# Layers written out, six parts of output, level products round the row groups: one change to a two-layer encoder step on Trainium2

## The reference

```python
def trunk_layer(x, ...):
    x = layer_norm(ALPHA * x + 0.5 * swiglu(x, w_ffn1_in, w_ffn1_out), g[0], b[0])
    mix, ... = token_mixing(x, ...)
    x = layer_norm(ALPHA * x + mix, g[1], b[1])
    x = layer_norm(ALPHA * x + memory_attend(x, mem_k, mem_v, w_q, w_o), g[2], b[2])
    return layer_norm(ALPHA * x + 0.5 * swiglu(x, w_ffn2_in, w_ffn2_out), g[3], b[3])

def token_mixing(x, ...):          # one projection x @ w_in feeds all three branches
    y_pool = pool_mixer(...)       # trailing means over 2, 4, 8, 16 tokens
    y_mla  = ...                   # 8 heads of attention over compressed keys, block-causal mask
    y_gla  = gla_mixer(...)        # 4 heads of 32: gated linear attention, A = sum q * decay * k
    m = g_a * (y_pool @ w_a) + g_b * (y_mla @ w_b) + g_c * (y_gla @ w_c)
    return m @ w_out

def swiglu(x, w_in, w_out):
    gate, up = split(x @ w_in)     # inner width 2816
    return (silu(gate) * up) @ w_out
```

## Time and profile before

| | |
|---|---|
| median of 3 runs | 3059.01 us (3057.55 to 3063.16) |
| profiled execution | 3057.24 us, span 3055.5 us |
| granted TensorE clock, mean | 0.989 of full speed |
| busy, share of the span | TensorE 96%, GpSimd 36%, VectorE 35%, ScalarE 30% |
| chain that ended last | TensorE 88%, VectorE 5%, ScalarE 2%, issue 2% |
| DMA | 259.8 MB, mean 85 GB/s |

### The profile page before, as it was taken

One profiled execution on the slowest core, in us unless ns is written; L12 is line 12 of the kernel. 1 busy time (PEld: TensorE's weight loads), 2 busy tenths in 40 slices (PEclk: granted clock), 3 DMA queues, 4 the chain that ended last, 5 costly groups with the idle time before them and its releaser, 6 DMA issues.

```text
span 3055.5 us, 54729 instructions
## 1 busy us (share of the span) xinstructions
PE 2936.7 (96%) x22374; PEld 2813.5 (92%) x22374; DVE 1069.3 (35%) x1864; ACT 917.1 (30%) x1404; POOL 1087.8 (36%) x454
## 2 busy tenths in 40 slices
PE   7999999899999999999999999999999999999996
PEld 7999998699998799999999999877999988999995
DVE  3111245643435461112331121566434254511123
ACT  2222243322334252222332221533223342422223
POOL 3343323034362234434333434321333622333431
PEclk9999999999999999999999999999999999999998
DMA  3222222022252022222222222211222511222222
GB/s 140 90 83 89 90 76 81 22 78 84 83 194 76 30 82 90 83 88 90 77 87 88 84 90 88 75 64 36 78 83 85 199 56 53 73 89 89 83 90 85
DMA packets 74436, 259.80 MB, mean 85 GB/s; under 512 B 10704, under 2 KB 13648, under 8 KB 72848
## 3 DMA queue, kind: packets, MB, share of 16 engines
q1 hardware_dynamic: 65520, 238.58, 24.1%
q10 hardware_dynamic: 8736, 18.64, 1.7%
HBM read 249.32 MB, written 7.87 MB: 84 GB/s over the span
## 4 chain that ended last, share of the span: by engine, by line
PE 88%; DVE 5%; issue 2%; ACT 2%; DVEq 2%; ACTq 1%
PE PS L320 87%; DVE XL L1320 1%; DVE Y L1320 1%; ACT Y L923 1%; DVEq L1395 0%; DVE PT L1635 0%; DVE SC L1610 0%; ACT LNT L923 0%; ACT WH L923 0%; DVE P L1625 0%; DVE O L1323 0%; DVE LNT L1320 0%; DVE LNT L1323 0%; DVEq L1810 0%; PE PS L590 0%
## 5 line engine op out<-in xcount | busy, mean ns | idle before, releaser
L310 POOL TENSOR_TENSOR WL<-WR,WH 128x1024 fp32r<-128x1024 f32 x450 | 1087.6, 2423 | 1911.4 <-ACT WH L923 1911.0
L320 PE MATMUL PS<-XH,WH 128*128 128x272 f32 x4192 | 927.1, 292 | 49.3 <-DVE XL L1320 40.3
L320 PE MATMUL PS<-XL,WH 128*128 128x272 f32 x4192 | 915.6, 290 | 0.0
L320 PEld LDWEIGHTS PS<-XH,WH 128*128 128x128 f32 x4192 | 679.3, 189 | 68.8 <-DVE XL L1320 52.4
L923 ACT ACTIVATE WH<-WR 128x1024 fp32r<-128x1024 f32 x455 | 479.6, 1056 | 726.7 <-DMA WR<-in_w 708.0
L320 PEld LDWEIGHTS PS<-XL,WH 128*128 128x128 f32 x4192 | 680.1, 190 | 0.0
L320 PE MATMUL PS<-XH,WL 128*128 128x272 f32 x4192 | 651.2, 289 | 0.0
L320 PEld LDWEIGHTS PS<-XH,WL 128*128 128x128 f32 x4192 | 576.7, 189 | 0.0
L1320 DVE TENSOR_TENSOR LNT<-LNT,PS 128x544 f32<-128x544 f32 x88 | 63.4, 721 | 796.1 <-PE PS L320 759.0
L923 ACT ACTIVATE LNT<-PS 128x544 f32<-128x544 f32 x138 | 85.9, 622 | 719.4 <-PE PS L320 719.2
L320 PE MATMUL PS<-HL,WH 128*128 128x272 f32 x1408 | 299.1, 289 | 0.0
(11 more groups left out here) (222 smaller groups left out, 2849.5 us busy)
## 6 DMA issues: line engine op xcount, KB each, us to landing
WR<-in_w SPq DMA_DIRECT2D x455, 512.0 KB, 3.5
Y<-in_x ACTq DMA_DIRECT2D x4, 544.0 KB, 11.8
out_y<-Y ACTq DMA_DIRECT2D x1, 2176.0 KB, 6.6
MRAW<-in_mem ACTq DMA_DIRECT2D x2, 1024.0 KB, 4.8
MKs<-in_memk_in ACTq DMA_DIRECT2D x2, 1024.0 KB, 6.0
MVs<-in_memv_in ACTq DMA_DIRECT2D x2, 1024.0 KB, 9.0
out_mem_k<-MKp ACTq DMA_DIRECT2D x2, 1024.0 KB, 6.0
out_mem_v<-MVp ACTq DMA_DIRECT2D x2, 1024.0 KB, 8.0
```

The lines of the kernel that those rows point to most:

```text
L310: pool.tensor_tensor(WL[s][:, :], WR[s][:, :], WH[s][:, :].bitcast(F32), ALU.subtract).then_inc(lo_ready[s], 1)
L320: return pe.matmul(out, lhsT, rhs, start=start, stop=stop, skip_group_check=True)
```

## The change

Seven edits, most of them to the order of the work.

**1. Layers written out.** The outer loops of TensorE, ScalarE and VectorE become Python loops, so that each layer has its own instructions; the inner loops stay. `norm_last(l, 3, 1)` goes from the end of a layer into the `quad` of the next layer's `f1i`; only the last layer's stands alone.

```diff
-            with pe.Fori(0, L) as l:
-                ffn_in(l, "f1i", 4 * l)
+            for l in range(L):
+                ffn_in(l, "f1i", 4 * l, (lambda: norm_last(l - 1, 3, 1)) if l else None)
...
                 ffn_out(l, "f2o", 4 * l + 3, l * 2 + 1)
-                norm_last(l, 3, 1)
+            norm_last(L - 1, 3, 1)
```

```diff
+Y_PARTS = [(0, 0, 4), (0, 4, 4), (1, 0, 4), (1, 4, 2), (1, 6, 1), (1, 7, 1)]
...
-            for s in range(AHEAD):
-                sp.wait_ge(w_used[s], L * ROUNDS + 1)
-                sp.dma_start(WR[s][:, :], io["w"][0, s]).then_inc(landed[s], 16)
+            for h, c, n in Y_PARTS:
+                sp.wait_ge(S["y_fin"], 16 * (4 * L - 1) + 8 * h + c + n)
+                sp.dma_start(io["y"].rearrange("p (c t) -> p c t", c=KC)[:, c:c + n, hs(h)],
+                             Y[:, c:c + n, hs(h)]).then_inc(S["st_y"], 16)
...
-            act.wait_ge(S["y_fin"], 16 * 4 * L)
-            act.dma_start(io["y"], Yf[:, :]).then_inc(S["st_y"], 16)
```

```diff
-            for h in (0, 1):
-                for s in (0, 1) if h == 0 else (2, 3, 4):
-                    convert(0, s)
-                for c in range(KC):
...
+            load_x(0)
+            act.preload_act_table_set("silu_and_others")
+            convert(0, 0)
+            x_hi(0, 0)
+            convert(0, 1)
+            convert(0, 2)
+            load_x(1)
+            x_hi(0, 1)
+            convert(0, 3)
+            convert(0, 4)
+            x_hi(1, 0)
+            x_hi(1, 1)
...
             for i in range(16):
+                for s in {0: (0,), 2: (1,), 4: (2,)}.get(i, ()):
+                    ve.wait_ge(hi_ready[s], 1)
+                    tt(WL[s][:, :], WR[s][:, :], WH[s][:, :].bitcast(F32), ALU.subtract).then_inc(lo_ready[s], 1)
```

```diff
-                    for h in range(4):
-                        r = slice(32 * h, 32 * h + 32)
-                        if sample:
-                            m_ = mm(PS[0:NS, 4 + h, 0:NS], a[r, NP_:T], b[r, NP_:T], True, True)
-                        else:
-                            for i in range(4):
+                    for i in range(1 if sample else 4):
+                        for h in range(4):
+                            r = slice(32 * h, 32 * h + 32)
+                            if sample:
+                                m_ = mm(PS[0:NS, 4 + h, 0:NS], a[r, NP_:T], b[r, NP_:T], True, True)
+                            else:
                                 m_ = mm(PS[:, 4 + h, i * 128:(i + 1) * 128], a[r, i * 128:(i + 1) * 128],
                                         b[r, i * 128:(i + 1) * 128], True, True)
```

```diff
                     act.wait_ge(S["pt_mm"], l * 8 + h + 1)
...
+                    f(PT[:, 0:512], PS[:, 3 * e, :], ACT.Copy)
...
-                    ve.tensor_copy(PT[:, 0:1024].rearrange("p (b t) -> p b t", b=2),
-                                   PS[:, 3 * e:3 * e + 2, :]).then_inc(S["pt_d"], 1)
+                    ve.tensor_copy(PT[:, 512:1024], PS[:, 3 * e + 1, :]).then_inc(S["pt_d"], 1)
...
+                    normalize(h)
+                    if h:
                         out_lo(h - 1)
-                    normalize(h)
```

```diff
                 normalize(0)
-                normalize(1)
                 queries(4)
                 turned(0)
+                normalize(1)
                 queries(5)
...
                 maxima(3)
+                normalize(3)
                 out_lo(2)
-                normalize(3)
                 turned(3)
```

More of the change, by code:

```diff
@@ L294, in _ @@
         def _(sp):
-            with sp.Fori(0, L * ROUNDS) as q:
+            for s in range(SLOTS):
+                sp.wait_ge(w_used[s], 1)
+                sp.dma_start(WR[s][:, :], io["w"][0, s]).then_inc(landed[s], 16)
+            sp.dma_start(TAB[:, :], io["tab"]).then_inc(S["const_in"], 16)
+            sp.dma_start(CST[:, :], io["cst"]).then_inc(S["const_in"], 16)
+            sp.dma_start(LN_[:, 0:1024], io["mask"]).then_inc(S["const_in"], 16)
+            with sp.Fori(1, L * ROUNDS) as q:
                 for s in range(SLOTS):
@@ L298, in _ @@
                     sp.dma_start(WR[s][:, :], io["w"][q, s]).then_inc(landed[s], 16)
-            for s in range(AHEAD):
-                sp.wait_ge(w_used[s], L * ROUNDS + 1)
-                sp.dma_start(WR[s][:, :], io["w"][0, s]).then_inc(landed[s], 16)
+            for h, c, n in Y_PARTS:
+                sp.wait_ge(S["y_fin"], 16 * (4 * L - 1) + 8 * h + c + n)
+                sp.dma_start(io["y"].rearrange("p (c t) -> p c t", c=KC)[:, c:c + n, hs(h)],
+                             Y[:, c:c + n, hs(h)]).then_inc(S["st_y"], 16)
+            sp.wait_ge(S["st_y"], 16 * len(Y_PARTS))
         @block.gpsimd
         def _(pool):
-            with pool.Fori(0, L * ROUNDS) as q:
+            for s in range(FIRST, SLOTS):
+                pool.wait_ge(hi_ready[s], 1)
+                pool.tensor_tensor(WL[s][:, :], WR[s][:, :], WH[s][:, :].bitcast(F32), ALU.subtract).then_inc(lo_ready[s], 1)
+            with pool.Fori(1, L * ROUNDS) as q:
                 for s in range(SLOTS):
@@ L932, in convert, with load_x, x_hi @@
                 f(WH[s][:, :], WR[s][:, :], ACT.Copy).then_inc(hi_ready[s], 1)
[L934 to L949 removed]
+            def load_x(h):
+                for i in (0, 1):
+                    act.dma_start(Y[:, 4 * i:4 * i + 4, hs(h)],
+                                  io["x"].rearrange("p (c t) -> p c t", c=KC)[:, 4 * i:4 * i + 4, hs(h)]).then_inc(
+                        S[f"x_in{2 * h + i}"], 16)
+            def x_hi(h, i):
+                act.wait_ge(S[f"x_in{2 * h + i}"], 16)
+                for c in range(4 * i, 4 * i + 4):
+                    f(XH[:, ch(c, h)], Yf[:, ch(c, h)], ACT.Copy).then_inc(S["x_hi"], 1)
+            load_x(0)
[10 more added lines that the diff above has]
+            x_hi(1, 1)
+            for l in range(L):
                 done = [AHEAD - 1]
@@ L997, in layer_norm @@
                 def layer_norm(n, j, c0):
+                    last = n == 4 * L - 1
                     def rstd(h):
@@ L1008, in chunk @@
                         act.wait_ge(S["ln_d"], 16 * n + 8 * h + c + 1)
-                        f(XH[:, ch(c, h)], Yf[:, ch(c, h)], ACT.Identity, scale=g, bias=b)
+                        if not last:
+                            f(XH[:, ch(c, h)], Yf[:, ch(c, h)], ACT.Identity, scale=g, bias=b)
                         f(Yf[:, ch(c, h)], Yf[:, ch(c, h)], ACT.Identity, scale=g, bias=b).then_inc(S["y_fin"], 1)
@@ L1018, in layer_norm @@
                             square_last(j, 1)
-                        if c == 3:
+                        if c == 3 and not last:
                             hi_to(c0 + 3)
@@ L1023, in layer_norm @@
                         chunk(1, c)
-                        if c == 0:
+                        if c == 0 and not last:
                             hi_to(c0 + 4)
@@ L1028, in ffn_out @@
                     c0 = CBASE[name]
+                    ahead = min(c0 + 24, L * CHUNKS - 1 - l * CHUNKS)
                     for c in range(20):
-                        hi_to(c0 + c + 4)
+                        hi_to(min(c0 + c + 4, ahead))
                         for m in range(KC - 1):
@@ L1033, in ffn_out @@
                                 square(n, m)
-                    hi_to(c0 + 24)
+                    hi_to(ahead)
                 def proj_out(l, name, n):
@@ L1396, in layer_norm @@
                         mul(h, c)
-                        if c:
+                        if c and not last:
                             lo(h, c - 1)
@@ L1402, in layer_norm @@
                             head(1)
-                    lo(h, KC - 1)
+                    if not last:
+                        lo(h, KC - 1)
             ve.memset(XH[:, KC * T:].bitcast(F32), 0.0)
@@ L1419, in _ @@
             ve.drain()
-            with ve.Fori(0, L) as l:
+            for l in range(L):
                 def gated(b, x):
```

14 lines of the change are left out of this document (2 added, 12 removed).

## The result

The changed kernel takes **2979.68 us** (median of 4 runs, 2978.99 to 2980.57) against 3060.07 us before (median of 4, 3057.55 to 3063.16): a ratio of 0.9739, 95% interval 0.9727 to 0.9751, 80.4 us less. The forecast was 2977 us, with a range of 2964 to 2997. The total is close, and hides one term that was almost wholly wrong.

The account below looks back on a forecast made before the run. TensorE, busy 2936.7 of 3055.5 us, was taken as the bound. Terms summing to 82.1 us came off the profiled 3057.2 us, and 1.8 us was added for the median: 2977 us, range 2964 to 2997.

Parts of the forecast that it names:

- Level products: 16 level calls: changing head after every matmul lets row groups overlap, 1.5 us saved a call, 24.0 us, bounds 0 and 26.
- The rival of pairs: Level calls: only two row groups run together, so 10.9 us gained instead of 24.0, total 2990 us; chance 0.16.
- Attention: Attention over heads: earlier normalising and a copy split between VectorE and ScalarE save 12.4 us, bounds 6 and 15.
- The rival that the ring closes elsewhere: Attention keeps its length: a head's cycle from scores to next scores is held elsewhere, waits only renamed; 2989 us, chance 0.11.
- Memory: Memory stage: earlier low-part subtraction removes 7.7 us of waits and 4.2 us lost at low clock, less 0.6: 11.3 us.
- the two bank releases that now stand behind the subtraction: Memory stage: releases formerly behind VectorE's low-part subtraction, which moves behind the fifth chunk; may cost 0.3 us each.
- Cross attention: Cross attention: waits for the fifth query group's copy, 5.6 us, and the last head's weights, 3.2 us, go: 8.8 us.
- Turn: Between the layers: without the loop, 34.05 us becomes 31.86 as where sums are woven into the next stage; 2.2 us.
- Head: Kernel start: earlier weight conversions and low parts let TensorE start at 13.4 instead of 20.50 us; 7.0 us, bounds 5 and 8.5.
- Tail: Kernel end: first half 3.8 us earlier, last normalisation 4.9 us less, output in parts 4.3 less; 13.0 us, bounds 11 and 14.
- Slower by reading code: Rival: reading in the second layer's code starves TensorE; at 10 ns a matmul more than the gain is lost, 3089 us; chance 0.02.
- Clock: Half-clock stretches after two level calls and in the second layer's attention and cross attention: half of 6.8 us, 3.4 us gained.

Follow-up runs that it names:

- woven copies: Changed kernel with VectorE's first two memory-key copies moved into its gaps waiting for ScalarE in chunks 6 and 7: 2971.3 us, 8.3 less than the changed kernel.
- the order by pairs: Changed kernel with level products alternating between heads 0 and 1 through all four blocks, then heads 2 and 3: 2987.0 us, 7.3 more than the changed kernel.

## Why the prediction was right, and where it was wrong

- **Level products: right in mechanism, the size a little low.** Taken were 1.5 us a call, measured 1.64 in each of 16, 26.3 us, the upper bound. 1.1 us a layer is given back at one place that the forecast had called free of waits: behind the first call TensorE now waits 0.84 us for ScalarE, which the longer call had covered.

```profile
640.12 0.52 PE L337 MATMUL PS<-BH,WH 128*128 128x272 f32 x2 [0.84 <-ACT LNT L940]
```

  The two stretches at half the clock behind level calls, 1.5 us each, are gone and lie in this row: 26.3 - 2.2 + 3.0 = 27.1, and 0.2 in the products between. The rival of pairs falls: four groups run side by side. The ratio of 3.07 times from the Trainium skill, "TensorE: Matmul & The Clock Gate", section "Part 3: Packing small matmuls", is not reached by this trace: the call's length fell by 2.82 / 1.17 = 2.4 times, with 128 columns where the page has 512. Nor did the strict order that the section states lead to two at a time: in the new order the records of four groups start 7 ns apart in the trace.
- **Attention: right in the whole, one part too large.** 12.4 forecast, 13.5 measured, of which 1.9 is what the second layer gained more than the first; before had a stretch at half the clock there. The order of normalising is 7.0 us when undone (7). The copy is 5.8 in the medians (5.5), but some 4 in the trace, where the low parts give back 1.8 us: the forecast named them as late next and priced them only in its lower bound. The wait before the values is 1.20 us (1.1 forecast). The rival that the ring closes elsewhere falls for these edits; with the whole copy on ScalarE the waits do change their name to the low parts.
- **Memory: wrong, 2.1 instead of 11.3 us.** The step that failed is the price of "the two bank releases that now stand behind the subtraction", 0.3 us each. It priced what the subtraction adds to the releases, and not how late they are against the time at which TensorE would want the bank: without the old wait it would reach the third group of keys at 858.0 us (its last gate product ended at 852.3, two groups take 5.7), while VectorE's first copy of keys came at 862.18 us, and the part of that delay that the subtraction made was at most 2.3 us. The trace of before had this row:

```profile
862.18 0.42 DVE L1826 COPY MKp<-PS 128x256 f32<-128x256 f32 x1
```

  The stall had hidden it. The answer to what is late next stood seven rows further down VectorE's timeline than the subtraction; woven copies then gave 8.3 of the missing 9.2 us. The clock term of 4.2 us inside the 11.3 went with it, since each new stop brings its own 3.4 us at half the clock.
- **Cross attention: right,** 9.3 against 8.8, with 1.5 of it from the clock; 1.2 us of waiting for the last weights (`CP`) stay. No run undoes this edit alone; the stage's length and the waits that went are the evidence.
- **Turn: the size right, the reason wrong.** 2.5 us against 2.2, but the comparison of 34.05 with 31.86 us was put down to the missing weaving. The loop's own turn did it, with the stretch at half the clock behind it; the weaving is worth nothing.
- **Head: right,** 12.47 us against 13.4, as VectorE began the third low part at 10.9 us and not at 12.1; 0.5 us is given back by slower first matmuls. **Tail: right in its parts:** from the second root to the last block 8.07 us (8.0), from there to the end 2.4 instead of 7.05 (4.3 less forecast, 4.65 measured), the first half 4.3 us earlier (3.8). The two parts undone singly cost 7.1 and 4.7 us in their traces, 11.8 of 13.8; the two conversions of weights that are gone, 1.04 us each before, would fill the rest, an estimate that no run tries.
- **Slower by reading code: out,** as the run with loops written out and the second layer's equal times show.
- **Clock.** A term of its own, 3.4 us, was too small: outside the memory stage and the turn, half clock has a share of about 6.4 us in the rows above (3.0 + 1.9 + 1.5), nearly all of the 6.8 that the forecast halved.
- **The range.** The stated bounds and the whole clock term add up to 10.5 us below the forecast, 2966 us and not 2964.

In sum the forecast had 82.1 us and the two traces show 76.7: memory 9.2 too much, levels 3.4 too little, head, attention, cross attention, turn and tail together 3.2 too little, the clock's 3.4 counted in the rows, other stages 0.7. The medians differ by 80.4 us, more than the traces, because the profiled execution of before lies 2.8 us below its median, and that of the changed kernel 0.9 us above. So the range held, but the nearness of 2977 to 2979.7 is partly luck: terms missed in opposite directions, and half of the 5.4 us that the traces are short of the sum are hidden by which executions were profiled.

## What to carry to other kernels

When a wait is taken away, look in the old trace for when the waiting engine would want its next three or four inputs and outputs' banks, and for when those come: a stall can hide another engine's lateness that stands behind it, as the 3.9 us for the low part hid the late bank here. Small matmuls on different rows of the array should go round all four row groups, not stay in one for a block and not alternate between two. Compare two traces by the same matmul's number, stage by stage: where medians scatter by several us, this shows single edits to a tenth.

## What the runs showed of the hardware

- **The next row group starts before the one ahead is through.** A head alone needs 0.11 us a record. In the old order the next head started when the fifth of eight records had started (0.55 us), in the order by pairs the second pair too (1.65 = 0.55 + 1.10 us), and a call of the old order is 3 x 0.55 + 1.10 = 2.75 us. Whether what counts is the records left, or something else that takes 0.55 us, was not tried with another length.
- **The clock fell behind old level calls, with TensorE busy all along.** In the three traces with the old order (before, loops written out, old order put back) 11 of 48 level calls are followed by a stretch at 1.2 GHz and 1.5 us of delay, with no wait near it; in the ten traces with the new order none of 160, nor in the 16 calls by pairs. Windows of TensorE, loops written out, behind a call that ended at 662.5 us:

```profile
662.93:666.34 3.41, 3.41 (x17) 0.50 0.02 5
```

  Which calls it hits changes from run to run. The times of the kernels with the old order lie 4 to 11 us apart, those of the changed kernel 1.6; but its edits with the new order bring 1 to 7 us of scatter, so it is not the only source. What the chip counts there was not tried.
- **The turn of the outer loop held TensorE for 3.49 us**, once in a span of 3055.5 us; the turns of the inner loops, which lie between products, show no such wait.
